# Moving the weight matmuls' operands to multiples of 512 bytes in SBUF

## What is computed

```
# first block
proj = rms_norm(x) @ w_in                      # 2048 x (5632 + 24 gates)
mix  = concat(diff_attention(...), nsa_attention(...))
x    = x + rms_norm(mix @ w_out)               # 2048 x 2048
u    = causal_dwconv(rms_norm(x) @ w_up)       # 2048 x 11264
x    = x + rms_norm((gelu(gate) * up) @ w_down)  # 5632 x 2048
# second block
u    = rms_norm(x) @ hgrn_w_in                 # 2048 x 10240
x    = x + rms_norm(gated_recurrence(u) @ hgrn_w_out)
u    = dwconv3(rms_norm(x) @ ffn_w_in)
x    = x + rms_norm((silu(gate) * val) @ ffn_w_out)
```

## Time and profile before

| | |
|---|---|
| median of three runs | 2729.57 us |
| the profiled execution | 2735.14 us |
| its span, first to last instruction | 2733.4 us |
| TensorE matmul busy | 2634.4 us, 96% |
| VectorE busy | 1620.8 us, 59% |
| ScalarE busy | 1357.8 us, 50% |
| mean granted TensorE clock, as a share of 2.4 GHz | 0.969 |
| read from HBM | 458.40 MB, 170 GB/s over the span |

### The profile page before, as it was taken

How to read it: one execution, slowest core, us unless ns; L and a number is a source line. 1 busy time by engine, 2 the same in 40 slices (tenths; PEclk the granted TensorE clock), 3 DMA queues, 4 the chain that set the end, 5 groups by cost and what they waited for, 6 DMA issues and landing times.

```text
span 2733.4 us, 37125 instructions
## 1 busy us (share of the span) xinstructions
PE 2634.4 (96%) x13482; PEld 2112.3 (77%) x13482; DVE 1620.8 (59%) x1856; ACT 1357.8 (50%) x1785; POOL 194.8 (7%) x92
## 2 busy tenths in 40 slices
PE   8799788999999999999999999999999999999998
PEld 6688656878888887888787878878788888887886
DVE  4344663556666666544548587695566666665444
ACT  4344553455555555333454544545555555554342
POOL 1000000001112121100000000000011112121000
PEclk9899865999999999999999999999999999999999
DMA  8866310555666665655565555554566666555554
GB/s 200 234 190 185 114 55 29 180 155 177 183 184 178 183 181 165 211 189 186 161 190 166 169 170 155 155 163 162 154 192 177 177 183 184 178 183 194 190 185 138
DMA packets 242450, 465.01 MB, mean 170 GB/s; under 512 B 14344, under 2 KB 23345, under 8 KB 241841
## 3 DMA queue, kind: packets, MB, share of 16 engines
q1 hardware_dynamic: 240001, 453.44, 54.5%
q0 software_dynamic: 2240, 10.21, 1.8%
q10 hardware_dynamic: 112, 0.03, 0.0%
HBM read 458.40 MB, written 5.23 MB: 170 GB/s over the span
## 4 chain that ended last, share of the span: by engine, by line
PE 94%; DVE 2%; ACT 2%; DMA 1%; issue 1%; SPq 0%; DVEq 0%; ACTq 0%
PE acc L219 29%; PE acc L220 29%; PE acc L221 28%; DMA raw<-in_w_in_dram 1%; PE tp L462 1%; PE tp L960 1%; PE tp L265 1%; PE tp L1296 1%; PE acc L924 1%; DVE wlo L206 1%; PE tp L1324 1%; PE tp L941 1%; PE tp L1275 0%; PE tp L962 0%; DVE x L432 0%
## 5 line engine op out<-in xcount | busy, mean ns | idle before, releaser
L206 DVE TENSOR_TENSOR wlo<-raw,whi 128x1024 fp32r<-128x1024 f32 x856 | 1148.6, 1353 | 940.4 <-ACT whi L201 938.3
L201 ACT ACTIVATE whi<-raw 128x1024 fp32r<-128x1024 f32 x856 | 904.1, 1060 | 1102.0 <-PE acc L221 1039.5
L219 PE MATMUL acc<-whi,ahi 128*128 128x512 f32 x2656 | 1062.0, 400 | 21.4 <-DVE wlo L206 14.5
L220 PE MATMUL acc<-wlo,ahi 128*128 128x512 f32 x2656 | 1051.1, 396 | 0.0
L221 PE MATMUL acc<-whi,alo 128*128 128x512 f32 x2656 | 1050.9, 396 | 0.0
L219 PEld LDWEIGHTS acc<-whi,ahi 128*128 128x128 f32 x2656 | 499.8, 188 | 142.0 <-DVE wlo L206 22.7
L221 PEld LDWEIGHTS acc<-whi,alo 128*128 128x128 f32 x2656 | 499.0, 188 | 122.3
L220 PEld LDWEIGHTS acc<-wlo,ahi 128*128 128x128 f32 x2656 | 499.9, 188 | 116.5
L219 PE MATMUL acc<-whi,hhi 128*128 128x512 f32 x704 | 278.2, 395 | 0.0
L220 PE MATMUL acc<-wlo,hhi 128*128 128x512 f32 x704 | 278.1, 395 | 0.0
L221 PE MATMUL acc<-whi,hlo 128*128 128x512 f32 x704 | 278.1, 395 | 0.0
(11 more groups left out here) (208 smaller groups left out, 1304.7 us busy)
## 6 DMA issues: line engine op xcount, KB each, us to landing
raw<-in_w_up_dram SPq DMA_DIRECT2D x176, 512.0 KB, 3.8
raw<-in_ffn_w_in_dram SPq DMA_DIRECT2D x176, 512.0 KB, 4.1
raw<-in_hgrn_w_in_dram SPq DMA_DIRECT2D x160, 512.0 KB, 3.7
raw<-in_w_in_dram SPq DMA_DIRECT2D x88, 512.0 KB, 3.7
raw<-in_w_down_dram SPq DMA_DIRECT2D x88, 512.0 KB, 4.3
raw<-in_ffn_w_out_dram SPq DMA_DIRECT2D x88, 512.0 KB, 4.3
raw<-in_w_out_dram SPq DMA_DIRECT2D x32, 512.0 KB, 4.3
raw<-in_hgrn_w_out_dram SPq DMA_DIRECT2D x32, 512.0 KB, 4.0
```

The lines of the kernel that those rows point to most:

```text
L201: act.activation(whi[:, s, :], raw[:, s, :], ACT.Copy).then_inc(hi_done, 1)
L206: dve.tensor_tensor(wlo[:, s, :], raw[:, s, :], whi[:, s, :].bitcast(F32), ALU.subtract).then_inc(lo_done, 1)
L219: pe.matmul(out[:, t, :], xh, whi[:, s, c], start=(kt == 0), stop=False)
L220: pe.matmul(out[:, t, :], xh, wlo[:, s, c], start=False, stop=False)
```

## The change

A tile of 96 float32 (384 bytes in each partition) is asked for ahead of `raw`, and one of 72 (288 bytes) behind `psq`, the last of the small tiles that live through the whole program. No instruction reads or writes either. Every tile of the program gets a new address: those from `raw` to `psq` lie 384 bytes further on, all later ones 672 bytes. Offsets inside tiles, instructions, waits and transfers stay as they are.

```diff
@@ -67,6 +67,7 @@
             return made[name]
 
 
+        sb("pad_front", [P, 96])
         raw = sb("raw", [P, RING, CK * GC])
         whi = sb("whi", [P, RING, CK * GC], F32R)
         wlo = sb("wlo", [P, RING, CK * GC], F32R)
@@ -78,6 +79,7 @@
         prs = sb("prs", [P, 4, NT])
         prime = sb("prime", [P, 1])
         psq = sb("psq", [P, 4, NT, NG])
+        sb("pad_end", [P, 72])
 
 
 
```

## The result

The changed kernel is faster: 2669.22 us, the median of four runs (2665.78 to 2672.78), against 2729.81 us before, taken with them (four runs, 2729.5 to 2730.5). The ratio is 0.9778, 95% interval 0.9761 to 0.9795, so 56 to 65 us less. The forecast was no change; what came is rival 2, whose price was 2663 us. How far that price was earned is said further down.

A forecast was written before the change was run, and what follows sets the result against it. TensorE's rate on 10,080 weight matmuls at 233.3 ns was taken as the bound; 0 for the matmuls plus 0 for the rest left the median unchanged at 2729.5 us (chance 0.70), range 2715 to 2763 us (0.84).

The forecast's parts named there:

- rival 2: Weight matmuls speed up in part, as moving and stationary reads disturb each other by relative residue: 2663 us, chance 0.10.
- What bounds the kernel: TensorE's rate on 10,080 weight matmuls of `products`, 233.3 ns each: 2352 us, 86% of the 2733.4 us span.
- The sum: 0 for matmuls and 0 for the rest; profiled execution 5.6 us above the median, put down to profiling; forecast 2729.5 us.
- That the excess has nothing to do with neighbours: Weight matmuls keep 233.1 ns in their last 8 us, where VectorE, ScalarE, GpSimd and DMAs do nothing.
- It grows with columns, not with boundaries crossed: Line 735's 256-column matmuls take 117.4 ns against 233.3 for 512: ratio 1.99, where block crossings would give 1.67 or 1.8.
- Residue 352 and residue 128 feed alike: Line 879 streams 256 columns from residue 128 in 113 to 118 ns, like line 735 from 352; matmul gain taken as 0.
- A stationary operand at residue 0 is already there: In `blkhl`, block l = 22 starts at 5632 = 11 x 512; its chunk takes 117 ns, no quicker than others.
- Rival 4: Relative-residue mechanism with sign reversed: weight matmuls slow to 236.6 ns, + 33 us, 2763 us; chance 0.12.
- Rival 1: The weight matmul stream speeds up wholly to 213.6 to 216 ns, 2531 to 2553 us; chance 0.05.
- Rival 3: DMA stretches of the first 100 us shrink by more than 5.5 us: 2720 us; chance 0.03.
- the costs at 0: Transposes, float32 attention matmuls, the hidden split of lines 201 and 206, and DMAs into `raw`: each taken as 0 change.
- The bound of 2.0 us: Most the second DMA stretch on the chain could give: what TensorE lacks in the full-speed stretch behind it, 20 - 17.99.

The follow-up runs named there:

- e5_end224: Kernel before plus only a 224-byte pad behind the small tiles (moving residue 128, stationary 64): 2690.19 us, ratio 0.9836.
- e2_end160: Kernel before plus only a 160-byte pad behind the small tiles (moving residue 128, stationary 0): 2723.99 us, ratio 0.9968.
- the maps: Kernels running only lists of matmuls at chosen operand residues, in place of the program; one execution each; 226.7 ns a matmul at pair (0,0).
- m2_fine: Matmuls only, 36 per residue pair, differences 0 to 256 bytes in 4-byte steps, then fewer columns; 512 columns: 226.7 ns at 0, 236.7 at 4.
- e1_front: Kernel before plus only the 384-byte front pad (moving residue 0, stationary 224): 2731.95 us, ratio 0.9997.
- e7_diff96: Kernel before plus pads of 64 bytes in front and 192 behind (moving residue 192, stationary 96): 2731.58 us, ratio 0.9996.
- the first map: Matmuls only, 12 per pair of residues from 0 to 480 in 32-byte steps, in place of the program: 226.7 ns at (0,0), 233.3 at (352,128).

## Why the prediction was wrong, step by step

**What bounds the kernel** was right, and so was the exchange rate: 10,080 matmuls times the change in the distance gives 67 us for the changed kernel (a little over the 56 to 65 of the interval), 44 for e5_end224 (44.2 measured) and 8 for e2_end160 (8.6). The sum's remark that profiling costs 5.6 us is not shown: the profiled execution of the changed kernel, 2669.63 us, lies at its median, and executions of the kernel before ran from 2725.9 to 2736.1 us in the later comparisons. As the sum compared median with median, nothing hung on it.

**That the excess has nothing to do with neighbours** was right: the maps have it with no other engine at work.

**"It grows with columns, not with boundaries crossed"** is a step that failed. I compared line 735 with the weight matmuls and took the ratio 1.99 as proof of a rate that no address changes. The two cases differ in more than columns: line 735 loads 24 and 48 columns at residues that step by 192 bytes. m2_fine shows that at 256 columns difference 0 is even slower than 32 (120.8 against 118.1 ns), so nothing could be read from 256 to 512. Line 735 itself depends a little on addresses, as its 115.8 ns after the change show. The ratio of nearly 2 was a coincidence.

**"Residue 352 and residue 128 feed alike"** is the step that set the forecast: on it the cost of the excess that addresses could give back was put at 0, and it measured 6.6 ns a matmul. It failed in its question. I looked at one operand's residue at a time and asked whether either counts. Neither does by itself in e1_front and e2_end160; their difference does, modulo 256, and it was -224, that is 32, for all 10,080 weight matmuls. "For 128-column loads the trace has one single value" was no evidence against an effect of addresses: the trace had one single difference, so it could show no variation. I noted that and gave the weight to the wrong side.

**"A stationary operand at residue 0 is already there"** was true and beside the point for the same reason: its difference to the moving residue 128 was no multiple of 256. The rows from which I took 0 were all of 256 columns.

**Rival 2** had the mechanism (two reads that disturb each other by their relative residue) and its price from the quick chunk of line 879 in the earlier trace rows: 113 x 2 = 226.7 ns. The 512-column distance is that, and the time 2669 instead of 2663. That the price fits so exactly is luck: line 879 loads 30 or 60 columns and streams 256, where m2_fine has 120.8 ns at difference 0, and after the change no chunk of that line is that quick (115.8 to 120.0 ns a chunk, mean 117.1 as before). The rival had 0.10 because I held the spread of 113 to 118 ns for noise of how a chunk begins; whether it was more than that stays open. Rival 4, the same mechanism with the other sign, meets its price of 236.6 ns, in series of one pair, only between the 32-byte steps: difference 4 costs 236.7 ns. Among the steps of 32 bytes, in which tiles are placed, the difference before was already one of the slow ones, and e7_diff96, the slowest in the first map, is no slower in the program.

**Rival 1 and the rule beside it.** The Trainium skill, "TensorE: Matmul & The Clock Gate", section "Back-to-back issue gap", has 216 ns for 512 columns at the full clock, which it calls the gap of an isolated matmul; for a stream of loads and matmuls it has about 131 ns. The maps run such streams and agree with the 216 for bfloat16 (215 to 217); none comes near 131, and in F32R none goes below 226.7. So the placement was 6.6 ns of the excess over 216, and the other 10.7 no address and no shorter load tried here gives back.

**Rival 3 and the costs at 0** (transposes, attention, splits, DMAs): the zeros held. The group that moved most is the split of line 206, 2.6 us of busy time more and hidden; the pieces of rival 3 grew by 0.1 and 1.4 us instead of shrinking. The bound of 2.0 us took the stretch of 80 to 100 us for one at full speed, though its granted clock is 0.82; as nothing was gained there, this did not matter.

## What to carry to other kernels

Where a stream of 512-column F32R matmuls at the full clock stands at 233 ns, look at the addresses of the moving operand and of the stationary operand that is loaded beside it, modulo 256 bytes, and shift one tile until they are equal (both at multiples of 32 bytes, as here); 32 bytes did it in this kernel, and the 512 bytes of the change's description did not matter. When a trace shows one constant value, ask what else is constant before taking the value as the hardware's: it says nothing on a quantity that never varied. And a comparison row must match in the size of both operands, since at 256 columns equal residues were no longer the quickest ones.

## What the runs showed that I had not expected

- For F32R, 128-column loads and 512 columns, at residues that are multiples of 32 bytes, the distance depends on the difference of the two addresses with a period of 256 bytes: 226.7 ns at 0, 228.9 at 64, 233.1 at 32. Between those residues the difference alone no longer says it: differences of 28, 60, 156, 236, 240 and 252 bytes from stationary residue 0 have about 226.7 to 227.1 ns as well, while both operands at residue 4, difference 0, have 237.6. What in the chip makes this pattern stays open.
- The load running beside the stream seems to count, and not the matmul's own stationary operand (229.7 against 236.7 ns); the series in which one operand alternates show that this is not all.
- bfloat16 operands of the same columns show none of it.
- Short series mislead: 12 matmuls of difference 96 gave 234.6 ns (last ten), 36 gave 233.3, the program 233.4. Both operands at 160 gave 228.8 in the series of 12 and 226.7 in the program.
